# A deeper set of rounded weight buffers in the expert stage of a float32 two-block network

## The reference, cut to what matters

```python
logits = xt @ router_w + router_b            # 32 experts, 4 per token
top_v, top_e = lax.top_k(logits, TOP_K)
gate = softmax(top_v)
for each expert e, on the tokens that chose it:
    hb = xb @ w1[e] + b1[e]                  # w1: 1024 x 2048
    g = minimum(hb[:, :1024], 7); u = clip(hb[:, 1024:], -7, 7)
    y = ((u + 1) * g * sigmoid(1.702 * g)) @ w2[e] + b2[e]   # w2: 1024 x 1024
out[token] += gate * y
...
bias = rpb[:, row difference, column difference]
s_win = where(col_ok, q @ k * scale + bias, -1e30)
```

## Time and profile before

| | |
|---|---|
| time, median of 3 runs | 2906.81 us (2906.61 to 2908.82) |
| the profiled execution's own time | 2904.19 us |
| its span | 2902.0 us, mean granted clock 0.97 |
| PE, DVE, ACT, POOL busy | 95%, 73%, 53%, 0% |
| DMA | 776 MB, mean 267 GB/s, 375 GB/s in the turns |

### The profile page before, as it was taken

How to read it: one execution, slowest core, us unless ns; L and a number is a source line. 1 busy time by engine, 2 the same in 40 slices (tenths; PEclk the granted TensorE clock), 3 DMA queues, 4 the chain that set the end, 5 groups by cost and what they waited for, 6 DMA issues and landing times.

```text
span 2902.0 us, 43416 instructions
## 1 busy us (share of the span) xinstructions
PE 2758.6 (95%) x17494; PEld 2471.4 (85%) x17494; DVE 2113.6 (73%) x1872; ACT 1534.3 (53%) x1294; POOL 11.0 (0%) x7
## 2 busy tenths in 40 slices
PE   5999998999999999999998899999999999999998
PEld 4888886778777777777786899999979999999998
DVE  5435547999999999999998968777446766754453
ACT  0023226888888888888885334334444434332342
POOL 0000000000000000000000100000000000000000
PEclk8999997999999999999999899999999999999999
DMA  9753336999999999999997677677516767755452
GB/s 376 249 180 125 132 132 246 378 375 375 364 373 364 376 377 378 380 379 380 376 376 274 189 262 271 247 257 247 204 38 217 276 248 245 274 179 175 146 189 72
DMA packets 172400, 776.07 MB, mean 267 GB/s; under 512 B 12112, under 2 KB 37712, under 8 KB 121328
## 3 DMA queue, kind: packets, MB, share of 16 engines
q1 hardware_dynamic: 168352, 767.08, 70.2%
q10 hardware_dynamic: 3920, 7.11, 0.8%
HBM read 773.10 MB, written 1.05 MB: 267 GB/s over the span
## 4 chain that ended last, share of the span: by engine, by line
PE 62%; DVE 21%; issue 13%; ACT 3%; DVEq 1%; DMA 0%; ACTq 0%; SPq 0%
PE psum L1195 36%; DVE w_low L2259 11%; PE psum L1149 7%; PE psum L1570 4%; PE psum L1335 4%; ACT w_high L917 2%; PE psum L1607 2%; PE psum L1274 2%; DVE mod_sums L1844 1%; PE psum L1543 1%; DVE arena L2278 1%; PE psum L1293 1%; PE psum L1383 1%; DVE arena L2291 1%; DVE hid L2293 1%
## 5 line engine op out<-in xcount | busy, mean ns | idle before, releaser
L2259 DVE TENSOR_TENSOR w_low<-ring,w_high 128x2048 fp32r<-128x2048 f32 x396 | 882.1, 2287 | 40.2 <-ACT w_high L917 36.2
L917 ACT ACTIVATE w_high<-ring 128x2048 fp32r<-128x2048 f32 x396 | 736.9, 1906 | 90.3 <-PE psum L1570 88.4
L2395 DVE TENSOR_TENSOR w_low<-ring,w_high 128x2048 fp32r<-128x2048 f32 (+1 forms) x199 | 432.7, 2184 | 325.8 <-ACT w_high L1011 322.6
L1011 ACT ACTIVATE w_high<-ring 128x2048 fp32r<-128x2048 f32 (+1 forms) x199 | 362.3, 1829 | 576.9 <-PE psum L1195 501.2
L1195 PE MATMUL psum<-h_high,w_high 128*128 128x256 f32 x2080 | 592.6, 285 | 28.9 <-ACT h_high L1024 21.0
L1195 PE MATMUL psum<-h_high,w_low 128*128 128x256 f32 x2080 | 594.8, 286 | 0.0
L1195 PE MATMUL psum<-h_low,w_high 128*128 128x256 f32 x2080 | 592.1, 286 | 0.0
L1195 PEld LDWEIGHTS psum<-h_high,w_high 128*128 128x128 f32 x2080 | 403.9, 194 | 31.2 <-issue 22.9
L1195 PEld LDWEIGHTS psum<-h_low,w_high 128*128 128x128 f32 x2080 | 398.7, 193 | 0.0
L1195 PEld LDWEIGHTS psum<-h_high,w_low 128*128 128x128 f32 x2080 | 397.9, 191 | 0.0
L1570 PE MATMUL psum<-w_high,xg 128*128 128x512 f32 x1056 | 347.4, 410 | 16.5 <-DVE w_low L2259 11.4
(11 more groups left out here) (278 smaller groups left out, 3289.2 us busy)
## 6 DMA issues: line engine op xcount, KB each, us to landing
ring<-in_exp_w SPq DMA_DIRECT2D x396, 1024.0 KB, 7.7
ring<-in_ffn_w SPq DMA_DIRECT2D x135, 1024.0 KB, 5.3
ring<-in_mod_w SPq DMA_DIRECT2D x96, 1024.0 KB, 5.5
ring<-in_ffn_w SPq DMA_DIRECT2D x40, 768.0 KB, 4.7
ring<-in_w_in SPq DMA_DIRECT2D x24, 1024.0 KB, 8.9
ring<-in_even_w_in SPq DMA_DIRECT2D x12, 1024.0 KB, 7.0
ring<-in_conv_w_in SPq DMA_DIRECT2D x12, 1024.0 KB, 5.0
ring<-in_w_branch SPq DMA_DIRECT2D x6, 1024.0 KB, 5.0
```

Of the source, the lines that this page charges most:

```text
L917: act.activation(high_ap(j, D), slot_ap(PLAN.moe_slot + j), ACT.Copy).then_inc(sem("expert_high_ready" + c.x), 1)
L1011: act.activation(high_ap(m, cols), slot_ap(s, 2, cols), ACT.Copy).then_inc(sem("w_high_ready"), 1)
L2259: dve.tensor_tensor(low_ap(PLAN.moe_slot + j, D), slot_ap(PLAN.moe_slot + j), high_ap(j, D).bitcast(F32), ALU.subtract).then_inc(sem("expe ...
L2395: dve.tensor_tensor(low_ap(s, cols), slot_ap(s, 2, cols), high_ap(m, cols).bitcast(F32), ALU.subtract).then_inc(sem("w_split"), 1)
```

## The change

There are seven edits.

1. The experts' high parts get six buffers (`MOE_HIGHS = 6`): the four of before and two more, which lie where the normalised tokens (`hT`) and the context (`cT`) were. `high` waits for TensorE's end with slot j - 6. The ring keeps eight places.
2. Both splitting engines run two slots further ahead: every group of `high` and of `low` has its numbers raised by two, a turn ends with slots 0 to 5 of the next, and the other instructions keep their places between the groups.
3. The product of bias and gates is no longer made ahead of the loop but in the additional turn (`biases`), into the PSUM of the result. `acc` is filled with zeros at the end of the mixer. `gateT` and `b2_rows` lie elsewhere. Two of three filler units fall away.
4. ScalarE splits slot 0 before it exponentiates the logits, and slots 1 to 5 before it copies the gathered tokens.
5. The sixteen fills become eight at the end of the mixer and one copy.
6. The squares of the gain are made in the additional turn, in `add_over`.
7. VectorE adds the column mask, just ahead of the neighbourhood scores, and GpSimd no longer does. The context is loaded after the expert stage, ahead of the position table on the same queue.

```diff
-RING2, HIGHS = 8, 4
+RING2, HIGHS, MOE_HIGHS = 8, 4, 6
...
-NEXT_SLOTS = tuple(range(TURN_SLOTS, TURN_SLOTS + HIGHS))
+NEXT_SLOTS = tuple(range(TURN_SLOTS, TURN_SLOTS + MOE_HIGHS))
...
+        def expert_high(j):
+            n = j % MOE_HIGHS
+            v = w_high[:, n, :] if n < HIGHS else (hT_high if n == HIGHS else cT_high)[:, 0, :]
+            return v.rearrange("p (k n) -> p k n", k=2)
...
-            pool.tensor_tensor(view, view, mask, ALU.add).then_inc(sem("rpb_masked"), 1)
...
-            act.dma_start(cT, ins["ctxT"].rearrange("(k p) t -> p k t", p=P)).then_inc(sem("ctx_landed"), 16)
...
                 for j in slots:
-                    c.await_used(act, j - HIGHS)
+                    c.await_used(act, j - MOE_HIGHS)
                     c.await_slot(act, j)
...
+            high(first_turn(0), 0)
...
+            high(first_turn(0), 1, 2, 3, 4, 5)
...
-                high(c, 21, 22)
+                high(c, 23)
+                if not last:
+                    high(c, *NEXT_SLOTS[:1])
                 rows("down0", "y_rows0", 1.0 / ALPHA)
                 c.await_unit(act, "gather0")
                 gathered(0, c.unit("gather0"), c.x)
-                high(c, 23)
                 if not last:
-                    high(c, *NEXT_SLOTS[:-1])
+                    high(c, *NEXT_SLOTS[1:-1])
                 rows("down1", "y_rows1", 1.0 / ALPHA)
                 c.await_unit(act, "gather1")
                 gathered(1, c.unit("gather1"), c.x)
...
+            act.dma_start(cT, ins["ctxT"].rearrange("(k p) t -> p k t", p=P)).then_inc(sem("ctx_landed"), 16)
             for r in range(ROWS):
...
+                def biases():
+
+                    await_freed(pe, U["gate_turn"])
+                    pe.wait_ge(sem("b2_landed"), 16)
+                    for k in range(DC):
+                        name = "result" + "b" * (k // 4)
+                        if k % 4 == 0:
+                            c.open_unit(pe, name)
+                        pe.matmul(c.unit(name)[:, (k % 4) * T:(k % 4 + 1) * T], b2_rows[0:N_EXPERTS, k * P:(k + 1) * P],
+                                  gateT[0:N_EXPERTS, :], start=(k % 2 == 0), stop=False, skip_group_check=True)
...
                 if over:
                     turn_rows("up0_turn", "up0", "up_rows")
+                    biases()
                     down(0, range(DC), 8)
...
-                low(c, 4, 5, 6, 7, 8, 9, 10)
+                low(c, 6, 7, 8, 9, 10, 11, 12)
                 gate_half(0)
-                low(c, 11, 12, 13, 14, 15)
+                low(c, 13, 14, 15, 16, 17)
                 up_half(0)
-                low(c, 16, 17, 18)
+                low(c, 18, 19, 20)
                 gate_half(1)
-                low(c, 19)
+                low(c, 21)
 
                 select(lambda at: small[:, bass.ds(c.columns + (at + 2), 2)], c.x, steps.link)
                 up_half(1)
-                low(c, 20, 21, 22, 23)
+                low(c, 22, 23)
...
-            dve.wait_ge(sem("rpb_masked"), 1)
+            dve.wait_ge(sem("rpb_landed"), 16 * ROWS)
+            mask = const("col_mask")[:, None, :].broadcast_to([P, TB * 8 * ROWS, GRID_W])
+            view = area(15360, TB * 8 * ROWS, GRID_W)
+            link(dve.tensor_tensor(view, view, mask, ALU.add))
```

More of the change, by code:

```diff
@@ L342 @@
 MOD_BUFFERS, MOD_BUFFER_BEFORE = mod_buffers()
+assert MOD_BUFFERS[L1_MODS][0] not in MOD_BUFFERS[L1_MODS - 1]
 GAIN2_BUFFER = [b for b in range(MOD_SUMS) if b not in MOD_BUFFERS[L1_MODS]][0]
@@ L890, in _, with high @@
                 act.activation(h_nat_high[:, n, :], unit(u)[:, :], ACT.Copy).then_inc(sem("h_nat_high_ready"), 1)
+            for q in PLAN.high_before:
+                await_release(act, q)
+            def high(c, *slots):
+                for j in slots:
+                    c.await_used(act, j - MOE_HIGHS)
+                    c.await_slot(act, j)
+                    act.activation(expert_high(j), slot_ap(PLAN.moe_slot + j), ACT.Copy).then_inc(
+                        sem("expert_high_ready" + c.x), 1)
+            high(first_turn(0), 0)
             route = small[:, 0:448]
@@ L975, in experts @@
                     high(c, *NEXT_SLOTS[-1:])
-            high(first_turn(0), 0, 1, 2, 3)
+            for half in range(2):
+                await_unit(act, U["gather"] + half)
+                gathered(half, unit(U["gather"] + half), "")
             most = many(act)
@@ L1604, in result @@
                         name = "result" + "b" * (k // 4)
-                        if k % 4 == 0 and e == 0:
+                        if k % 4 == 0 and e == 0 and not over:
                             c.open_unit(pe, name)
@@ L2149, in add_to @@
                 return last, u
+            dve.memset(acc, 0.0)
+            for n in range(4):
+                for b in range(TB):
+                    at = 36 * b + N_EXPERTS + n
+                    last = dve.memset(small[:, at:at + 1], -(n + 1.0) * 1e37)
+            link(last)
             mods_of("w_out")
@@ L2244, in _ @@
             find_busiest()
-            for half in range(2):
-                u = U["bias_sum"] + half
-                await_unit(dve, u)
-                free(dve.tensor_copy(acc[:, 4 * half:4 * half + 4, :], chunks(u)), u)
-                await_freed(dve, u)
             for name in PLAN.pads:
@@ L2268, in acc_to_x, with squared_gains @@
                 done(last)
+            def squared_gains():
+                for k in range(DC):
+                    gain = vec("final1")[:, k:k + 1]
+                    last = dve.tensor_scalar(mod_sums[:, GAIN2_BUFFER, k * P:(k + 1) * P], ones, gain, gain, ALU.mult, ALU.mult)
+                link(last)
+                link(dve.tensor_scalar(mod_sums[:, GAIN2_BUFFER, :], mod_sums[:, GAIN2_BUFFER, :], 1.0 / D, None, ALU.mult))
             def experts(c, steps, last=False, over=False):
@@ L2345, in _ @@
                 steps.leave(PAIRS)
-            for k in range(DC):
-                gain = vec("final1")[:, k:k + 1]
-                last = dve.tensor_scalar(mod_sums[:, GAIN2_BUFFER, k * P:(k + 1) * P], ones, gain, gain, ALU.mult, ALU.mult)
-            link(last)
-            link(dve.tensor_scalar(mod_sums[:, GAIN2_BUFFER, :], mod_sums[:, GAIN2_BUFFER, :], 1.0 / D, None, ALU.mult))
             experts(over_turn(busiest_expert(dve)), steps, over=True)
```

72 lines of the change are left out of this document (25 added, 47 removed).

## The result

The changed kernel takes **2915.75 us** (median of 7 runs, 2913.2 to 2927.03); the kernel before took 2906.81 beside it. The ratio is 1.0036, 95% interval 1.0022 to 1.0051: slower by 9 us, where 2902 was forecast and the range ended at 2914. A second measurement of it (experiment 12, whose profile is the second one of the table) gave 1.0038 (1.0025 to 1.0052). The chance given to slower was 0.14.

A forecast was written before the change was run, and what follows sets the result against it. VectorE's own work plus 1.6 us of waits a turn was taken to bound the kernel. Start -15.7, turns +26.4, additional turn -6.5 and mask -9.1 sum to -4.9, giving 2901.9 us; range 2869 to 2914.

The forecast's parts named there:

- What bounds the kernel, and the start: VectorE's work plus 1.6 us of waits a turn; before the turns, TensorE starts slot 0 at 451.2: -15.7 us.
- The turns: In the 16 expert turns, late landings of slots 8 to 12 lengthen each by 1.65 us: +26.4 us.
- The chain: Within a turn: slot 12 lands at 18.3, `select` ends 50.3, slot 20 starts 55.4, next slot 4 lands 62.5, end 68.7.
- the bound of +2.4 a turn: Upper bound for the turns: the whole landing wait and another 0.7 us for the two added wakes.
- slower: the clock: In the turns, TensorE's waits for hidden rows and `select` lower its clock: 2913 or 2944 us, chance 0.14.
- The additional turn: After the 16 turns: down projection begins 3.8 us earlier and runs at full clock, 2.7 less: -6.5 us.
- the 2.7: In the additional turn, the bias product closes the wait before the down projection, which then keeps full clock: -2.7 us.
- The mask: In the FFN after the experts, VectorE no longer slowed by GpSimd's mask addition: -9.1 us, bounds -6 to -10.
- The landing costs less: In the turns, engines fall back to the transfers' pace and a turn stays 67.2 us: 2875 us, chance 0.16.
- Half of it: In the turns, slot 12's landing costs but slot 4's doesn't hold the last down rows: 68.05, 2889 us, chance 0.17.
- The estimate beside the first of them: By the Trainium skill's page, slot 12 lands 1.9 us earlier, the sum about 32 us lower; that case near 2870.
- No wait is left: In the turns, VectorE never waits and a turn takes 65.6 us: 2850 us, chance 0.07.

The follow-up runs named there:

- experiment 12: The changed kernel unchanged, measured and profiled again: 2920.22 us.
- experiment 1: The changed kernel with six buffers kept but both splitting engines back to four slots ahead, in the order of before: 2866.45 us, ratio 0.9871.
- Experiments 5 and 6: The changed kernel, then the kernel before, each with one more 1 MB transfer a turn behind slot 8: 2943.57 us and 2907.98 us.
- experiment 4: The changed kernel with ScalarE's copy of the next turn's slot 4 moved behind the last down rows and the gathered tokens: 2902.62 us.
- experiment 7: The changed kernel with, in the additional turn, the up rows copied ahead of slots 10 and 11, which VectorE splits behind the hidden rows: 2911.57 us.
- experiment 8: The changed kernel without the bias product in the additional turn: 2913.68 us, ratio 1.0038.
- experiment 2: The changed kernel with four buffers and four slots of lead, everything else of the change kept: 2873.76 us, ratio 0.9897.
- experiment 10: The kernel of experiment 1 with the additional turn's order of experiment 7: 2864.66 us, ratio 0.9862.
- experiment 11: The kernel of experiment 10 with ScalarE copying next turn's slot 3 ahead of the last down rows and slot 12 ahead of the swish: 2846.56 us.
- experiment 9: The kernel before with only the mask addition moved from GpSimd to VectorE, the context still loaded ahead of the expert stage: 2895.05 us, ratio 0.9961.
- experiment 5: The changed kernel with one more 1 MB transfer a turn, inside DRAM, issued behind slot 8: 2943.57 us, ratio 1.0123.
- experiment 3: The changed kernel with five slots of lead, one less, and six buffers: 2878.17 us, ratio 0.9909.

## Why the prediction was wrong

Against its terms the two profiles of the changed kernel miss by -2.6 and +4.1 us at the start, +9.1 and +8.4 in the turns, +9.4 and +8.2 in the additional turn, +1.0 and -0.1 at the mask and +0.7 and +1.5 in the rest. The medians miss by 13.9.

- **What bounds the kernel, and the start.** Right. DVE's wait at slot 4 was the four buffers: with six and the old order it goes (experiment 1). Slot 0 began at 450.2 to 455.4 in the other kernels with this start, forecast 451.2. With the clock ahead of it taken out, the gain (14.4 and 14.5) is a good 1 us less than the 15.7 forecast and inside its bounds. The 448.6 is not a better change but a clock that happened to be higher ahead of it.
- **The turns.** The chain was right link by link: slot 12's landing (18.3), `select`, slot 20, slot 4 ahead of the rows. Experiments 5 and 6 show the first link, experiment 4 the last. Its size was a little low: the turn shown took 69.0, I used 68.85, and the mean was 69.21 and 69.38. That is 5.4 to 8.0 us in 15 turns, within the bound of +2.4 a turn. One part is the last link: in the first profile slot 4 landed 62.6 to 63.2 us after slot 0, where I had 62.5.

  The other part is the clock. The forecast held against the last rival that 2.9 us is shorter than the wait seen to lower it. In each of turns 2 to 16, in both profiles, TensorE waited 2.8 to 3.4 us for the first hidden rows, and in all but one of them the granted clock was half for 3.4 or 6.8 us near that wait; in the turn shown from 1047.30 on:

```profile
1047.30:1050.70 3.40, 3.40 (x9) 2.65 (x8) 3.40 (x3) 3.33 (x4) 0.00 (x0) 0.50 1.01 419
```

  So the mechanism of the rival "slower: the clock" was there in every turn, though I had argued against it. It cost little because the loss lies ahead of `select`, for which TensorE had to wait anyway: 0.4 to 0.7 us of that wait is left in the turns with 3.4 us of half clock, which take 69.15 and 69.11 as means of the two profiles, and none in those with 6.8, which take about 69.37. In the one turn left over, in the second profile, the half clock came behind `select`, and the turn took 71.93. The mean lies between my 68.85 and the rival's 69.55. The first turn added the rest, 3.8 us over its forecast in the first profile and 0.6 in the second; the 3.2 between them is the clock of one execution (experiment 12).
- **The additional turn.** This is the step that failed: -6.5 forecast, with bounds of -3 to -8, +2.9 and +1.7 measured. It is 8 to 9 us off and has the wrong sign, where the turns are as far off with the right mechanism; either of the two put right would have brought the median into the range. Three statements in it were false.

  "The last lands at 15.8": I took the spacing of a steady turn. Here slots 10 and 11 landed 14.9 and 17.3 after slot 0 (13.3 and 16.8 in the second profile). "Let their turn end at 20.5": ACT in the changed kernel, and then PE:

```profile
1575.90 1.91 ACT L901 ACTIVATE hT_high<-ring 128x2048 fp32r<-128x2048 f32 x1 [3.12 <-DMA ring<-in_exp_w]
1578.25 1.91 ACT L901 ACTIVATE cT_high<-ring 128x2048 fp32r<-128x2048 f32 x1 [0.43 <-DMA ring<-in_exp_w]
1580.07 1.01 ACT L926 ACTIVATE arena<-psum 128x1024 f32<-128x1024 f32 x1
```

```profile
1577.69 0.39 PE L1583 MATMUL psum<-consts,arena 128*128 128x128 f32 x2
1581.12 3.68 PE L1579 MATMUL psum<-consts,arena 128*128 128x64 f32 x16 [3.05 <-ACT arena L926]
1584.73 7.19 PE L1616 MATMUL psum<-arena,mod_sums 32*128 32x256 f32 x16
1591.85 1.22 PE L1564 MATMUL psum<-w_high,hid 128*128 128x512 f32 x2
```

  ACT stood before the landings of slots 10 and 11 (3.1 and 0.4 us) with the up rows ready behind it. PE idled 3.05, its clock fell, and the up turn and the product ran at half of it: 3.68, where this turn of rows took 1.90 before, and 7.19 where I had 3.6. VectorE was ready at 27.1, not at 23.7, and the down projection began at 31.0 instead of 24.1. Without the waits in that place (experiment 7) it begins at 22.9, so the 24.1 was in reach and the order kept it away; without the product (experiment 8) at 25.9. The third false statement is that the product keeps the clock up: in experiment 7 no wait is left, and the projection still begins at half clock. From the start of its first product to that of its last it took 9.8 us before, 9.6 and 8.5 in the two profiles of the changed kernel and 8.8 to 10.0 in experiments 1, 2, 7, 10 and 11: of the 2.7 at most 1.3 appeared.
- **The mask.** Right: -9.1 forecast, -8.1 to -9.2 in the stage, and by itself in experiment 9. In the kernel before it was one of the four instructions under GpSimd's addition that took 10.17 us, where the other three took 1.27 to 1.29 each. The four take 4.99 again, and nothing is late at the scores, where VectorE now adds the mask in 4.42 us and then still waits 14.37:

```profile
1637.24 4.99 DVE L1851 SCALAR_TENSOR_TENSOR mod_sums<-ring,cs,mod_sums 128x1024 f32<-128x1024 f32 x4
```

- **The rivals.** "The landing costs less" is out by experiment 5. "Half of it" is out by experiment 4, since the rows' copy was held by slot 4's landing. The estimate beside the first of them, that a landing 1.9 us earlier would take about 32 us off, should read 30 (16 x 1.9). "No wait is left" describes not this kernel but experiment 11, with 65.85 a turn against my 65.6. I never priced the buffers without the lead, and so did not see that only the lead costs.
- **The range.** It ended 1.75 us short. The forecast's own range had no room for the additional turn going backwards, though the trace of before had a row against it: there slot 11 of the additional turn landed at 17.2.

## What to carry to other kernels

A splitting engine that runs further ahead gains only until it meets the transfers. Compare, slot by slot, when it will arrive with when the slot lands, before adding lead; where buffers cause the wait, add buffers and leave the order. Ahead of a copy that the bottleneck engine waits for, put nothing that waits for a landing: the same mistake cost 0.9 us a turn here and 6 to 8 us in the one short turn. Look also at where in the turn TensorE's clock falls: ahead of a wait little of it showed (0.2 us a turn between 3.4 and 6.8 us of half clock), on the chain behind it 3.4 us cost 2 (experiment 3). After that the small waits of the engine that sets the turn are worth looking for one by one, since two moved copies gave 0.75 us a turn.

## What was unexpected in the hardware

- TensorE's clock fell without any wait. In experiment 7 no gap in its work from 1562 us on was longer than 0.1 us; the stretches of 1580 to 1584, 1584 to 1588 and 1588 to 1594 us:

```profile
1580.00:1584.00 4.00, 4.00 (x36) 3.89 (x36) 1.12 (x2) 1.47 (x3) 0.00 (x0) 1.00 1.02 420
1584.00:1588.00 4.00, 4.00 (x17) 2.92 (x17) 3.78 (x6) 4.00 (x3) 0.00 (x0) 0.88 1.02 411
1588.00:1594.00 6.00, 6.00 (x15) 4.70 (x16) 6.00 (x9) 0.17 (x1) 0.00 (x0) 0.51 0.56 193
```

  The granted clock goes from full (2.4 GHz) to half (1.2 GHz). What it did before: two turns of rows with 64 columns a product, and the bias product with 32 rows. Which of them matters was not tried. The same order does it again in experiment 11: its clock falls 24.0 us after slot 0 of the additional turn, with no gap over 0.1 us from 25 us ahead of that slot on.
- A transfer of 1 MB inside DRAM, put between two loads on the queue, took 7.1 to 7.4 us from issue to landing and delayed slot 12 by 1.6 us, in both kernels; the loads themselves land 2.5 us apart when the queue is full. Why it costs less than a load stays open.
- Slot 12 lands 18.1 to 18.4 us after TensorE's slot 0 (mean of ten turns) in all kernels without the added transfer, whatever the lead or the number of buffers: the landing follows TensorE's slots. The Trainium skill, page "DMA: Bandwidth & Descriptors", section "Anatomy of one DMA", has 2.0 us fixed and 436 GB/s, a fit that it gives for transfers that GpSimd issues, while SyncE issues these; with slot 8 issued at 2.4 an estimate by it is 16.4 for slot 12. The traces do not agree, and the measurement decides.
